# A decoder layer with 32 experts on one core: TensorE's next class read amid a body, passes in turn from both ends, modulation rows between two banks

## What is computed

```python
mod = silu(c) @ ada_w + ada_b
shift1, scale1, gate1, shift2, scale2, gate2 = split(mod, 6)
h = rms_norm(x, norm_mix_pre) * (1 + scale1) + shift1
x = x + gate1 * rms_norm(hybrid_mixer(h), norm_mix_post)
h = rms_norm(x, norm_ffn_pre) * (1 + scale2) + shift2
for e in range(32):                       # tokens that chose e
    hu = h[tokens_e] @ w_up[e] + b_up[e]   # 1024 x 2048
    y[tokens_e] += gate_e * (clamped_swiglu(hu) @ w_down[e] + b_down[e])   # 1024 x 1024
x = x + gate2 * rms_norm(y, norm_ffn_post)
```

## Time and profile before

| | |
|---|---|
| median of 3 runs | 1337.93 us (1336.8 to 1339.74) |
| the profiled execution's own time | 1338.13 us |
| its span | 1336.2 us |
| PE (products) busy | 1157.8 us (87%), 7951 records |
| PEld (weight loads) busy | 575.0 us (43%) |
| DVE busy | 312.0 us (23%) |
| ACT busy | 258.3 us (19%) |
| moved by DMA | 464.89 MB, mean 348 GB/s over the span |
| mean granted clock of TensorE | 0.952 |

### The profile page before, as it was taken

One profiled execution on the slowest core, in us unless ns is written; L12 is line 12 of the kernel. 1 busy time (PEld: TensorE's weight loads), 2 busy tenths in 40 slices (PEclk: granted clock), 3 DMA queues, 4 the chain that ended last, 5 costly groups with the idle time before them and its releaser, 6 DMA issues.

```text
span 1336.2 us, 21387 instructions
## 1 busy us (share of the span) xinstructions
PE 1157.8 (87%) x7951; PEld 575.0 (43%) x7952; DVE 312.0 (23%) x802; ACT 258.3 (19%) x395; POOL 0.2 (0%) x4
## 2 busy tenths in 40 slices
PE   5999899987989769988998988989988788788795
PEld 4745588744344324434343343342443233433233
DVE  2025445274111110202211121211111112111112
ACT  2135422123021111001112021111121111111112
POOL 0000000000000000000000000000000000000000
PEclk8899999997999898999999999999999989899898
DMA  9942565453789999549999999999999999999996
GB/s 356 380 168 94 200 243 218 161 228 148 290 342 416 418 417 418 215 164 420 416 418 417 419 414 417 417 419 418 417 418 419 417 417 417 417 418 418 419 417 271
DMA packets 102526, 464.89 MB, mean 348 GB/s; under 512 B 8188, under 2 KB 9556, under 8 KB 69590
## 3 DMA queue, kind: packets, MB, share of 16 engines
q1 hardware_dynamic: 100112, 460.47, 86.0%
q10 hardware_dynamic: 2374, 3.84, 0.8%
HBM read 463.24 MB, written 1.05 MB: 347 GB/s over the span
## 4 chain that ended last, share of the span: by engine, by line
PE 59%; DMA 26%; SPq 8%; DVE 4%; issue 3%; ACT 0%; DVEq 0%; ACTq 0%
PE psum L974 17%; DMA ring<-in_w_up 17%; PE psum L599 16%; PE psum L1047 9%; DMA ring<-in_w_down 8%; PE psum L908 5%; SPq L557 4%; SPq L552 3%; PE psum L966 3%; PE psum L1065 2%; PE psum L668 2%; DMA ring<-in_ada_w 1%; PE psum L605 1%; DVE area L1744 1%; PE psum L949 1%
## 5 line engine op out<-in xcount | busy, mean ns | idle before, releaser
L974 PE MATMUL psum<-ring,area 128*32 128x512 f32 (+2 forms) x2432 | 395.3, 627 | 45.2 <-DMA ring<-in_w_up 44.9
L974 PEld LDWEIGHTS psum<-ring,area 128*32 128x32 f32 (+2 forms) x2432 | 105.2, 122 | 329.4 <-issue 248.4
L1047 PE MATMUL psum<-ring,area 128*32 128x256 f32 (+2 forms) x2080 | 199.4, 422 | 30.1 <-DMA ring<-in_w_down 15.3
L908 PEld LDWEIGHTS psum<-area 128*128 128x128 f32 x1056 | 128.6, 202 | 31.1 <-issue 31.1
L908 PE MATMUL psum<-area 128*128 128x128 f32 x1056 | 135.2, 289 | 0.3 <-DVE area L1635 0.3
L1047 PEld LDWEIGHTS psum<-ring,area 128*32 128x32 f32 (+2 forms) x2080 | 71.8, 115 | 147.2 <-issue 79.6
L1704 DVE TENSOR_SCALAR area<-psum 128x256 f32<-128x256 f32 x51 | 21.7, 425 | 386.4 <-PE psum L974 386.4
L1257 ACT ACT_TABLE_LOAD x32 | 41.1, 1283 | 355.3 <-PE psum L949 355.3
L1269 ACT ACTIVATE area<-area 128x256 f32<-128x256 f32 x51 | 21.3, 417 | 400.0 <-DVE area L1704 400.0
L599 PE MATMUL psum<-ring,hT 128*128 128x512 f32 (+1 forms) x192 | 77.5, 559 | 0.0
L599 PE MATMUL psum<-hT,ring 128*128 128x256 f32 x320 | 71.1, 381 | 0.0
(11 more groups left out here) (201 smaller groups left out, 671.1 us busy)
## 6 DMA issues: line engine op xcount, KB each, us to landing
ring<-in_w_up SPq DMA_DIRECT2D x256, 1024.0 KB, 18.9
ring<-in_w_down SPq DMA_DIRECT2D x128, 1024.0 KB, 22.0
ring<-in_ada_w SPq DMA_DIRECT2D x12, 2048.0 KB, 16.4
ring<-in_w_in SPq DMA_DIRECT2D x10, 2048.0 KB, 13.2
ring<-in_w_out SPq DMA_DIRECT2D x2, 2048.0 KB, 10.2
ring<-in_w_in SPq DMA_DIRECT2D x3, 1024.0 KB, 15.7
ring<-in_w_branch_b SPq DMA_DIRECT2D x1, 2048.0 KB, 9.5
cst<-in_cst ACTq DMA_DIRECT2D x1, 1184.5 KB, 8.0
```

The source lines that it names most:

```text
L908: ins = pe.matmul(ps[banks[i]][:, kk % 4 * P:(kk % 4 + 1) * P], h2[:, tt, kk * P:(kk + 1) * P], S[:, tt, 0:P], start=(tt == 0 and kk % 4 = ...
L974: ins = pe.matmul(ps[b][g * P // G:(g + 1) * P // G, 0:w], XT[:, kk, t0:t0 + P // G], wt[:, c0:c0 + w], start=False, stop=kk == KT - 1, sk ...
L1047: ins = pe.matmul(ps[b][g * M:(g + 1) * M, 0:w], hidT[:, p, q * P + of * M:q * P + (of + 1) * M], down_weights(kk)[:, g * W + d * CW:g * W ...
```

## The change

Three edits, all on PE.

1. `ada_part` is split into `ada_rows(m)` and `ada_columns(unit, ms)`. The first half's rows come first as before. The second half's rows are issued within the first half of the projection: those of chunk 1 behind bank `sbq0`, those of chunk 3 behind bank `sbq1`. The columns stay where they were.
2. The units of the up products go forward for an even kk and backward for an odd one (kk = 0 to 5; the last two tiles stay unit by unit). The passes of the down products go backward for an even kk and forward for an odd one.
3. A register `pe_class` holds the next expert's class. It is loaded before the loop between the two banks of the first gather, and in every body right before the wait for the turned rows (`ht_read`), for expert e + 1. The top of the loop only compares the register. The wait for `order_ready`, which stood at the end of a body, stands before this load.

```diff
-            def ada_part(unit, ms):
-
-                for n, m in enumerate(ms):
-                    w = chunk(arrived(f"ada{m}"))
-                    fill(f"ar{m}", [(bank(f"ar{m}")[32 * (k % 4):32 * (k % 4) + 32, :], silu_rep[:, k * 32:(k + 1) * 32],
-                                     w[:, k, :], k < 4, k >= 4) for k in range(KT)])
+            def ada_rows(m):
+
+                w = chunk(arrived(f"ada{m}"))
+                fill(f"ar{m}", [(bank(f"ar{m}")[32 * (k % 4):32 * (k % 4) + 32, :], silu_rep[:, k * 32:(k + 1) * 32],
+                                 w[:, k, :], k < 4, k >= 4) for k in range(KT)])
+
+            def ada_columns(unit, ms):
                 un.wait_free(pe, unit)
                 for n, m in enumerate(ms):
                     un.wait_read(pe, f"ar{m}")
...
             steps = [chan_unit(f"sbq{m}", sbq, 2 * m) for m in range(2)]
+            for m in MOD_A[0]:
+                ada_rows(m)
             for half in range(2):
-                ada_part(f"ada_a{half}", MOD_A[half])
+                ada_columns(f"ada_a{half}", MOD_A[half])
...
                             ins = pe.matmul(o, l, r, start=i == 0 and k == 0, stop=last, skip_group_check=True)
-                    if half == 1:
+                    if half == 0:
+                        ada_rows(MOD_A[1][m])
+                    else:
                         ins.then_inc(bank_full[un.bank(f"sbq{m}")], 1)
...
+            next_class = nc.alloc_registers("pe_class", engines=[pe.engine])
+
             pe.wait_ge(first_slots, 1)
             gathers(FIRST_BANKS, 0)
+            pe.wait_ge(cls_ready, 1)
+            nc.regs_mov(next_class, class_at(pe, 0))
             gathers(FIRST_BANKS, 1)
...
             ins.then_inc(acc_done, 1)
-            pe.wait_ge(cls_ready, 1)
...
                     pe.wait_ge(up_tile[kk], 16 * e + 16)
-                    for u in range(n_u):
+
+                    for u in range(n_u) if kk % 2 == 0 else reversed(range(n_u)):
                         ins = up_step(u, kk)
...
+                pe.wait_ge(order_ready, 1)
+                nc.regs_mov(next_class, class_at(pe, e + 1))
                 pe.wait_ge(ht_read, MAX_T * e + MAX_T)
                 for kk in range(FT):
                     if kk % 2 == 0:
                         pe.wait_ge(dn_tile[kk // 2], 16 * e + 16)
-                    for p, (G, _) in enumerate(passes):
+                    for p in range(len(passes)) if kk % 2 else reversed(range(len(passes))):
+                        G, _ = passes[p]
...
                 ins.then_inc(acc_done, 1)
 
-                pe.wait_ge(order_ready, 1)
-
-            experts(pe, "pe", lambda e, root, again: [by_class(pe, class_at(pe, e), lambda k: body(e, k), "pe", root, again)])
+            experts(pe, "pe", lambda e, root, again: [by_class(
+                pe, nc.snap(next_class, min_val=0, max_val=NC - 1), lambda k: body(e, k), "pe", root, again)])
```

## The result

The changed kernel took 1326.38 us (median of 4 runs, 1325.43 to 1327.13) beside 1337.37 for the kernel before (4 runs, 1336.41 to 1339.74): a ratio of 0.9913 with a 95% interval of 0.9897 to 0.9928. Two later measurements gave 0.9929 (0.9915 to 0.9942) and 0.9920 (0.9907 to 0.9933), so 9.5 to 11.6 us is what there is to explain.

What follows compares the result with a forecast made beforehand. PE and transfers were taken to bound the kernel by turns, in a chain of four. Start +0.3, shape changes -3.2 and class loads -2.6 gave -5.5 us: 1332.4 us for the median, range 1329.0 to 1336.0.

Steps and rivals of the forecast that it cites:

- What bounds the kernel: Whole kernel: PE and the weight transfers set the pace by turns; only PE time outside the transfer-bound stretches counts.
- Four pieces: PE to the second expert's first up tile, transfers to about 503.7 us, PE into the eighth expert, transfers to the end.
- runs of transfers: The second and last stretches of the chain, about 378 to 504 us and 597 us to the end, where DMA sets the pace.
- whatever PE does there waits for tiles: From 597 to 1321 us DMA is busy throughout at 417 GB/s, so PE's work there was said to wait for weights.
- Passes from both ends: Up and down products of the first and seventh experts: fewer changes of weight shape, 3.2 us saved.
- The class in a register: Between bodies on PE: the class load leaves the path, 0.65 us four times, 2.6 us saved (bounds 1.8 and 2.8).
- the four ways: Entry, first expert to second, into the seventh and out of it: 0.65 us saved at each.
- Jumps that miss: Jumps out of the first expert and into the seventh begin to stall, 3.2 us each plus low clock: 1341.8 us; 5%.
- Rows between the banks: Projection at the start: nothing shortened, two more changes of weight shape, +0.3 us (0 to 0.4).
- The rival in which the clock stays up at the second gap: After the columns at the start, 6 us at half speed become 3: 1329.4 us; 10%.
- Sum: Whole kernel: the start's cost and the savings at the entry, first expert and seventh expert add to -5.5 us.
- the bound of 1330.5: Fastest time by the terms' bounds: 0.184 us for all 26 changes of shape (4.8) and no cost at the start.

Runs made afterwards that it cites:

- load_twice: The kernel before with the class loaded twice at the top of the loop; 1349.43 us, ratio 1.0074.
- turns_only: The kernel before with only the passes and units in turn from both ends; 1334.56 us, ratio 0.9972.
- rows_only: The kernel before with only the second half's rows moved between the projection's banks; 1337.34 us, ratio 0.9996.
- before_again: The kernel before, unchanged, measured again for a second profile; 1337.65 us, ratio 0.9999.
- after_third: The changed kernel, unchanged, measured a third time; 1326.97 us, ratio 0.9920.
- after_idle_c1: The changed kernel with three loads that nobody uses ahead of class 1's body; 1327.54 us, ratio 0.9921.

## Why the prediction was wrong, point by point

**What bounds the kernel: right.** Four pieces, of which PE sets two. The starts of the two runs of transfers moved and the last run kept its length. One clause was too strong: "whatever PE does there waits for tiles" is true for gains only; PE has 2 to 3 us to spare in three experts, and idle time added there can cost the clock as well (load_twice).

**Passes from both ends: right, undersized by a fifth.** Up 0.91 and 1.00 us for the 0.95 and 1.10 forecast. Down 1.01 and 1.01 for 0.59 and 0.56: I priced a change of shape in the down products at 0.08 us by what the joint passes take over the sum of single ones; measured are 1.01 / 7 = 0.144 us, near the 0.152 (0.91 / 6) and 0.167 (1.00 / 6) of the up products. At 0.144 the 15 changes are 2.2 us and not 1.26, so the single passes must hold some 0.9 us that the joint ones don't pay; what it is no run shows. Together 3.93 us for 3.2 in the chain; in the time of turns_only it is 2.75 us by the medians, with an interval of 2.1 to 5.2. The estimate from the Trainium skill (TensorE: Matmul & The Clock Gate, Single matmul latency), 0.166 us and 4.3 in all, lay nearer than my down price. That formula is for a single bf16 product, and these are float32, so it may be nearer by luck.

**The class in a register: the four ways right, their sum too.** 0.70 at the entry, 0.70 out of the first expert, 0.91 into the seventh, 0.36 out of it: 2.67 for 2.6. The last is small since the jump that misses took 3.81 us instead of 3.49. The load between gather and down products cost nothing that the chain shows. Jumps that miss stayed two, the one from the seventh expert and the first one, so that rival fell.

**Rows between the banks: nothing to be seen.** 0.9996 alone; from the first columns to the second 16.19 us in rows_only for 15.77 in before_again, both with one low stretch of the clock of 3.4 us: 0.4 for the 0.3 forecast. The rival in which the clock stays up at the second gap fell with it: where it stayed up, it did so in the old order too (turns_only).

**The step that failed: "Sum".** It has no term for the clock; I had it in rivals only, at the start and behind a missing jump. The seventh expert's extras ran at the low clock in the kernel before, and the register's 0.9 us of idle time less keeps most of it away. From gates to up it took 13.80 us in the mean of the four profiles with 1.9 us of idle time and the old order of the products (load_twice, with 2.5, left out), and 10.75 in the seven with 0.9 to 1.0 (after_third and after_idle_c1 taken in): 3.1 us. With it the sum becomes 0.4 - 3.9 - 2.7 - 3.1 = -9.3 us, and the unexplained 0.5 of the first run of transfers makes it 9.8; measured were 9.5 to 11.6 in three series. The row was there to be read: the window from 504 to 539 us has a clock of 0.90, and that expert's extras took 5.29 us, 16 products with 32 moving columns. What one profile could not show is that it is mostly more: low for some 7 us there, but for 10 to 13 in the other three. How much idle time it takes, and at what moment the clock falls, stays open. With 0.94 to 1.00 us of it the clock was low for some 3.4 us in five profiles and for 6.8 in two, and the kernel with 1.63 us had 6.8 as well.

Two slips in the prediction change nothing: the bound of 1330.5 takes 2.6 us for the loads, where the bound given for them is 2.8; and that the first gather ran at half clock is not in the rows cited for it, though the trace has it (0.50 from 313 to 319 us).

## What to carry to other kernels

Where idle time ahead of products with few moving columns is cut, look at the clock of what follows, and not only at the idle time: 0.9 us here was worth 4.0. Products with many columns that are due anyway could go ahead of them here, with a shorter low stretch (9.99 us for 13.80) or none (8.59 for 10.75). In a kernel of alternating bounds, find the few pieces where PE sets the pace before an edit is priced at "per expert", and ask in the other pieces how much slack there is: a gain there is waited away, but a loss beyond the slack is not (load_twice, 11.4 us).

## What was not expected of the hardware

PE counted as busy for all of 14.87 us with the granted clock at 0.56: behind 1.9 us of idle time it was low through all 16 products of 32 moving columns, 6.87 us, and came back amid the bias products. With two units of 512 columns ahead of them and the same idle time it was back before they began (9.99 us). And with the very same instructions the clock at the start fell for 6.8 us at both gaps in one profile, for 3.4 us at both in three, and for 3.4 us at the first alone in four (the eight profiles with the old order at the start), so that the first projection's last product began between 45.9 and 50.0 us.
